# Gate and up products of the experts, two output tiles at a time: high weights first, then low

## The reference

```
def expert_choice_ffn(h, w_router, w_gate, w_up, w_down):
    ...
    g, idx = lax.top_k(aff.T, cap)
    xs = flat[idx]
    hid = jax.nn.silu(jnp.einsum('ecd,edf->ecf', xs, w_gate)) * jnp.einsum('ecd,edf->ecf', xs, w_up)
    out = jnp.einsum('ecf,efd->ecd', hid, w_down) * g[..., None].astype(h.dtype)
    ...
```

## Time and profile before

| | us |
|---|---|
| median of 3 runs | 2164.92 (2163.8 to 2165.94) |
| the profiled execution | 2165.15 |
| its span, first to last instruction | 2162.9 |
| its mean granted clock of PE | 0.973 |

### The profile page before, as it was taken

The page is one execution under the profiler, slowest core; times in us unless marked ns, Lnnn a source line. Parts: engine busy times, 40 slices in busy tenths (PEclk is TensorE's granted clock), DMA queues, the critical chain, the costliest instruction groups (busy, mean ns, idle before and its releaser), DMA issues. The chain is left out here.

```text
span 2162.9 us, 43529 instructions
## 1 busy us (share of the span) xinstructions
PE 1996.9 (92%) x16048; PEld 1746.7 (81%) x16048; DVE 1450.8 (67%) x2601; ACT 1108.7 (51%) x1983; POOL 352.6 (16%) x587
## 2 busy tenths in 40 slices
PE   7999998899998998888899199999999999999996
PEld 6877876788787776677788199999999999999995
DVE  5366575666667666676258677777777777778875
ACT  5322322465566433366222066667666766667774
POOL 1213213000000122201221001111111111111233
PEclk9999999999999999999999599999999999999998
DMA  5211100100002222112232278777878887778995
GB/s 183 84 31 32 35 27 17 41 18 24 20 6 88 64 58 82 62 52 80 98 117 100 109 231 265 247 260 247 266 246 260 247 263 248 259 257 297 345 323 189
DMA packets 183465, 317.82 MB, mean 147 GB/s; under 512 B 11872, under 2 KB 82016, under 8 KB 183328
## 3 DMA queue, kind: packets, MB, share of 16 engines
q1 hardware_dynamic: 169984, 281.06, 38.5%
q0 software_dynamic: 8608, 30.68, 5.7%
q10 hardware_dynamic: 4736, 4.19, 0.7%
HBM read 279.97 MB, written 35.91 MB: 146 GB/s over the span
## 5 line engine op out<-in xcount | busy, mean ns | idle before, releaser
L2319 DVE TENSOR_TENSOR we_lo<-raw,we_hi 128x1024 fp32r<-128x1024 f32 x384 | 465.9, 1223 | 189.2 <-ACT we_hi L2244 188.4
L2210 PE MATMUL psum<-x_parts,we_hi 128*128 128x384 f32 x2048 | 585.5, 360 | 3.1 <-DVE we_lo L2319 3.1
L2212 PE MATMUL psum<-x_parts,we_lo 128*128 128x192 f32 x2048 | 513.6, 251 | 0.0
L2244 ACT CAST we_hi<-raw 128x1024 fp32r<-128x1024 f32 x384 | 400.1, 1054 | 157.0 <-PE psum L2212 93.7
L2212 PEld LDWEIGHTS psum<-x_parts,we_lo 128*128 128x128 f32 x2048 | 392.3, 192 | 0.6
L2210 PEld LDWEIGHTS psum<-x_parts,we_hi 128*128 128x128 f32 x2048 | 385.8, 188 | 4.1 <-issue 3.5
L599 PE MATMUL psum<-hT_hi,w_hi 128*128 128x512 f32 x512 | 213.8, 417 | 1.4 <-issue 0.7
L601 PE MATMUL psum<-hT_hi,w_lo 128*128 128x512 f32 x512 | 201.7, 394 | 0.0
L600 PE MATMUL psum<-hT_lo,w_hi 128*128 128x512 f32 x512 | 201.4, 393 | 0.0
L599 PE MATMUL psum<-hP_hi,w_hi 128*128 128x512 f32 x256 | 109.8, 429 | 16.5 <-DVE w_lo L572 12.2
L134 POOL TENSOR_TENSOR carried_pool<-minus_half 128x1 f32<-128x1 f32 x47 | 16.9, 359 | 635.3 <-ACT result_s L2286 489.6
(11 more groups left out here) (313 smaller groups left out, 3836.2 us busy)
## 6 DMA issues: line engine op xcount, KB each, us to landing
raw<-in_w_gate SPq DMA_DIRECT2D x128, 512.0 KB, 4.7
raw<-in_w_up SPq DMA_DIRECT2D x128, 512.0 KB, 6.9
raw<-in_w_down SPq DMA_DIRECT2D x128, 512.0 KB, 5.0
w_raw<-in_w_in SPq DMA_DIRECT2D x96, 256.0 KB, 2.8
y_rows<-x SPq DMA_DIRECT2D x12, 512.0 KB, 2.6
h_rows<-h SPq DMA_DIRECT2D x12, 512.0 KB, 2.9
y<-y_rows SPq DMA_DIRECT2D x12, 512.0 KB, 8.0
w_raw_s<-in_w_in SPq DMA_DIRECT2D x16, 256.0 KB, 3.1
```

The costliest lines, as they stand in the source:

```text
L2210: pe.matmul(out[:, 0:2 * SLOTS], w_hi[:, s, at], x_parts[p][:, k, :, :], start=(k == 0), stop=False, skip_group_check=True)
L2212: mm = pe.matmul(out[:, SLOTS:2 * SLOTS], w_lo[:, s, at], x_hi[p][:, k, :], start=False, stop=(k == DT - 1), skip_group_check=True)
L2244: act.copy(w_hi[:, n % PARTS, :], raw[:, s, :]).then_inc(hi.sem, 1)
L2319: dve.tensor_tensor(w_lo[:, n % PARTS, :], raw[:, n % RAW, :], w_hi[:, n % PARTS, :].bitcast(F32), ALU.subtract).then_inc(lo.sem, 1)
```

## The change

For each block `a` the four tiles are taken two at a time. For two tiles PE first makes both high products, then both low products, so the order is high, high, low, low where it was high, low, high, low. The two tiles write two banks, as before. Nothing else differs: the same products with the same operands, the same start and stop flags, the same waits, and the last product of a unit is still the low one of the fourth tile.

```
-                                for m in range(HALF):
-                                    at = slice(a * BLK + m * P, a * BLK + (m + 1) * P)
-                                    out = half(p, stage)[m]
-
-                                    pe.matmul(out[:, 0:2 * SLOTS], w_hi[:, s, at], x_parts[p][:, k, :, :], start=(k == 0),
-                                              stop=False, skip_group_check=True)
-                                    mm = pe.matmul(out[:, SLOTS:2 * SLOTS], w_lo[:, s, at], x_hi[p][:, k, :], start=False,
-                                                   stop=(k == DT - 1), skip_group_check=True)
+                                for m in range(0, HALF, 2):
+                                    pair = [(half(p, stage)[m + b], slice(a * BLK + (m + b) * P, a * BLK + (m + b + 1) * P)) for b in range(2)]
+                                    for out, at in pair:
+                                        pe.matmul(out[:, 0:2 * SLOTS], w_hi[:, s, at], x_parts[p][:, k, :, :], start=(k == 0),
+                                                  stop=False, skip_group_check=True)
+                                    for out, at in pair:
+                                        mm = pe.matmul(out[:, SLOTS:2 * SLOTS], w_lo[:, s, at], x_hi[p][:, k, :], start=False,
+                                                       stop=(k == DT - 1), skip_group_check=True)
```

## The result

The changed kernel took 2170.98 us (median of 16 runs, 2167.03 to 2179.14) against 2165.7 (16 runs of the kernel before beside them, 2162.31 to 2170.85). The ratio is 1.0022, 95% interval 1.0012 to 1.0031: slower by 2.6 to 6.7 us, about 0.2%.

What follows compares the result with a forecast made beforehand. PE was taken to set the pace, waiting for nobody. Steps of 174.5 ns high to high and 109.0 low to low, others unchanged, gave -0.8 ns per four, -0.8 us over 1024: 2165.15 - 0.8 = 2164.35, forecast 2164, range 2158 to 2170.

Steps and rivals of the forecast that it cites:

- Two loads of four: Weight loads in PE's expert stream: two of each four products' loads fall behind low products and come late, before and after.
- low to low: Step between two low products in the new order: 109.0 ns, between 105.8 and 111.7.
- high to low: Step from a high product to a low one in PE's expert stream: stays at 175.3 ns by the load steps.
- low to high: Step from a low product to a high one in PE's expert stream: stays at 109.0 ns by the load steps.
- The changes of bank: Every expert product now changes bank instead of every second one; costed at nothing.
- The half-clock fours: First expert products at 1.2 GHz, 533 ns a pair: made of the same two steps, they stay as they are.
- High to high: Step between two high products in the new order: 174.5 ns, the middle of 173.7 and 175.3.
- the loads did not run further ahead: Rival: in the new order loads start earlier and low products take 94 ns, 15 or 31 us less; chance 0.07.
- sums waiting for each other: Rival: low products wait for columns the high one just wrote; a four takes 545 ns, 25 us less; chance 0.04.
- The slower rival: Each switch from long to short product has its own price, 197 ns; a four takes 589, 21 us more; chance 0.06.
- The 0.07 for slower: Chance given to a slowdown beyond 0.2% (4.3 us): the slower rival plus the likeliest case's upper end.
- The estimate of 92 and 113 ns: Product times for 192 and 384 columns estimated from the skill page's 81 and 131 ns; 205 ns a pair.

Runs made afterwards that it cites:

- e10_alt: Kernel before, high and low still alternating, but every product goes to another tile and bank than the one before; 2166.47 us, ratio 0.9996.
- e13_onebank: Changed kernel with both tiles of a pair summed into one bank, which mixes their sums; 2170.94 us, ratio 1.0014.
- e1_again: The changed kernel run again with no edit, beside the kernel before; 2170.85 us against 2168.77, ratio 1.0017.
- e2_hllh: Order high, low, low, high over two tiles, against the kernel before's high, low, high, low; 2165.9 us against 2168.77, ratio 0.9992.
- e11_tile: Against the kernel before: both blocks of one tile behind each other, as high, low, low, high; 2168.22 us, ratio 1.0000.
- e17_hllh_apart: Against the kernel before: order high, low, low, high with neighbouring high and low products of different tiles; 2165.97 us against 2165.94, ratio 1.0000.
- e5_wide_hl: Kernel before, same order, but each low product streams 288 columns instead of 192; 2199.95 us, ratio 1.0155.

## Why the prediction was wrong

**What held.** PE set the pace, no wait came or went, and the whole effect of the edit lay in PE's stream. Two loads of four fall behind low products and are late. By the loads' starts low to low took 108.4 ns (forecast 109.0, between 105.8 and 111.7), and high to low and low to high together 284.5, as before (284.4). The changes of bank cost nothing (e10_alt, e13_onebank). The half-clock fours stayed (1066 ns in both traces).

**The step that failed** is "High to high". The prediction put it at 174.5 ns, between 173.7 and 175.3; it took 180.4 by the loads' starts, which is 5.9 more and 5.1 over the upper bound. The other three steps together came out 0.4 under their forecast. So the four took 573.3 and not 567.8, 2 ns over the upper end of 571.3. By the products' own starts the miss is larger: 200.0 from high to high, while high to low, which was to stay at 197, fell to 174.4. The prediction had itself read that the lateness belongs to whatever follows a low product. That is now the first of the two high ones, so its step is the long one; the two bounds came from products of 512 columns among their like and from a high product in front of a low one, and this step lies over both. In all, the sum said -0.8 us and the expert part gave +4.2; the rest of the way from 2164 to 2171 is that the median of before came out 0.8 higher over 16 runs, the rounding of 2164.35, and the spread of the two medians.

**Why it failed.** A step belongs to the cycle that it stands in and not to its two products. By the loads' starts a high product's step was 176.1 before, is 180.4 and 173.9 now, and 176.6 and 170.9 in the faster rhythm. Against the old order the two low steps cost 2.4 ns a four more (219.0 for 216.6), nearly the same in both rhythms; the two high ones cost 2.1 more in the slower one (354.3 for 352.2) and 4.7 less in the faster (347.5). The cycle of two high and two low so has two periods, 566.7 and 573.3, on either side of the 568.8 of the old order, and the changed kernel runs in the slower one in 15 of 16 runs of products (in all 16 of e1_again). Had it settled in the faster one throughout, 2.1 ns times 1024 would be some 2 us less than before, which a measurement of this kernel does not tell from no change; e2_hllh with its mixture shows just that.

**What stays open.** That the place where a run enters the cycle decides is shown; what in the engine keeps the two rhythms apart is not, nor whether and why one late load ends the faster one, nor why one such run of e2_hllh came back. The lower price of alternating lengths (10 against 13.3 ns) was measured without late loads, and how much of it is in the 4.4 ns could not be separated.

**The rivals.** No low product went at 94 ns by the loads' starts (108.4 and 110.6), and no load started before the product ahead of its own, so the loads did not run further ahead. The page "TensorE: Matmul & The Clock Gate" of the Trainium skill, section "Back-to-back issue gap", has loads and products pipelined through a 64-deep reorder window. The trace does not show such a depth: each load shown above is one product ahead and no more. No four came near 545 (sums waiting for each other). The slower rival had the right sign and the wrong mechanism: it wanted 197 ns from high to low, at the switch from a long to a short product, and by the products' starts just that step fell to 174.4, so that 589 was never seen. The long step went with the late load, to high to high. The 0.07 for slower was too little, because every term with its bounds came from a stream in another order.

**Slips without effect.** The 30 pairs of the earlier trace rows are the end of a run of sixteen units and not one unit. The load steps of the earlier trace rows are 176.1 and 108.3 ns, where the prediction has 175.3 and 109.0; their sum is right to 0.1. The estimate of 92 and 113 ns for 192 and 384 columns would be 89 and 114 on a straight line between the two figures that it starts from. The bounds of the sum with 1 us to each side give 2159 to 2169; the range was one wider on both sides.

## What to carry to other kernels

Where one engine is full and its instructions differ in length, the time of a step measured in one order does not carry to another order: give the whole cycle a margin of about 1% to both sides, also where every term has bounds (here orders of the same products took 566.7 to 576.6 ns where the old one took 568.8). Read the period over many repeats and in several runs of one trace, since one order can settle at two speeds; lay the loads beside what they load, since a wait of 0.07 us showed in no list of waits and yet a slower rest of the run followed it. And where an edit only rearranges a full engine's stream without taking work from it, expect a gain or a loss of tenths of a per cent, and measure the order's shifted forms beside it.

## What was not expected of the hardware

- One order of products has two settled periods, 566.7 and 573.3 ns for four (1.2% apart); each can last for whole runs. All of the difference lies in the high products. In 14 of 15 cases one load that came 0.07 us late was followed by the slower one (e2_hllh, e11_tile, e17_hllh_apart).
- Between products with no load late, 13.3 ns lie beside the stream when the neighbours are of one length (336 columns, 153.3 ns) and 10.0 when 384 and 288 columns alternate (300.0 ns for the two), but 13.3 also there in one run of e5_wide_hl.
- Settled periods come close to multiples of 6.67 ns: 153.3, 300.0, 566.7 and 573.3, and 616.6 and 568.8 over two and three fours (1233 and 1707 ns). This is an observation; no run tested it.
